# Where two cache copies and fourteen small loads stand in a two-layer decoder kernel

## The reference

```
layer 0: x += [conv module | gated delta rule](rmsnorm(x)) @ w_out_ab     # w_in_ab: 1024 x 3080
         x += PEER(rmsnorm(x))          # 8 heads, 16 of 16384 experts each, rows gathered from a table
         x += sigmoid(rmsnorm(x) @ w_gate) * (p @ w_emb)
layer 1: x += dilated_attention(rmsnorm(x)) @ w_out_c                     # 3 window groups, w_in_c: 1024 x 9216
         x += PEER(...); x += gate(...)
outputs: y, the conv and delta states, and for each window group the rolled key/value cache:
         bufs.append(concatenate([cache, kv_new])[:, L + T - keep:])
```

## Time and profile before

| what | value |
|---|---|
| median of 3 runs | 2553.03 us |
| profiled execution | 2553.16 us, its span 2551.4 us |
| TensorE matmul busy | 2052.6 us, 80% of the span |
| VectorE busy | 1281.3 us, 50% |
| ScalarE busy | 778.3 us, 31% |
| moved by DMA | 874.97 MB, mean 343 GB/s |
| copies of window 2048, 8 of them | 114.8 us to landing (median) |

### The profile page before, as it was taken

One profiled execution on the slowest core, in us unless ns is written; L12 is line 12 of the kernel. 1 busy time (PEld: TensorE's weight loads), 2 busy tenths in 40 slices (PEclk: granted clock), 3 DMA queues, 4 the chain that ended last, 5 costly groups with the idle time before them and its releaser, 6 DMA issues. The chain is left out here.

```text
span 2551.4 us, 25632 instructions
## 1 busy us (share of the span) xinstructions
PE 2052.6 (80%) x9026; PEld 1023.6 (40%) x9026; DVE 1281.3 (50%) x3157; ACT 778.3 (31%) x2275; POOL 644.4 (25%) x645
## 2 busy tenths in 40 slices
PE   5975796478887898877689999987887887988766
PEld 4764684253222243322244565454532222432222
DVE  0076653164776667765511031123556677666754
ACT  0143100023444344443411121121234444344443
POOL 0000000024443444434201000000344444454341
PEclk8987775789999999999789999999899999999978
DMA  6794999669999999999938755753899999999995
GB/s 208 265 336 155 330 329 339 246 263 392 427 427 427 427 427 411 427 427 427 421 151 321 273 206 205 286 206 124 326 427 427 427 427 427 427 425 427 427 427 246
DMA packets 129427, 874.97 MB, mean 343 GB/s; under 512 B 15876, under 2 KB 29700, under 8 KB 45195
## 3 DMA queue, kind: packets, MB, share of 16 engines
q0 software_dynamic: 92160, 662.74, 62.5%
q1 hardware_dynamic: 37139, 210.60, 23.3%
HBM read 861.98 MB, written 118.81 MB: 384 GB/s over the span
## 5 line engine op out<-in xcount | busy, mean ns | idle before, releaser
L1433 PE MATMUL tail_acc<-tail_ring,tail_diag 128*128 128x512 f32 x1216 | 596.8, 621 | 113.1 <-ACT tail_diag L1292 111.9
L1180 DVE CUSTOM_DVE_ANT_0 tail_ring<-tail_ring,all_h 128x1024 f32<-128x1024 f32 x344 | 418.7, 1222 | 239.8 <-DMA tail_ring<-in_peer_uv,tail_idx 239.3
L1573 POOL DMA_INDIRECT mid_wring<-in_peer_uv,tail_idx x232 | 239.1, 1031 | 1005.8 <-DVE all_x L1065 528.7
L1433 PE MATMUL tail_acc<-mid_wring,tail_diag 128*128 128x512 f32 x832 | 413.3, 624 | 98.7 <-ACT tail_diag L1292 98.4
L1573 POOL DMA_INDIRECT tail_ring<-in_peer_uv,tail_idx x344 | 368.7, 1072 | 478.6 <-PE tail_acc L1433 412.8
L1433 PEld LDWEIGHTS tail_acc<-tail_ring,tail_diag 128*128 128x128 f32 x1216 | 216.4, 192 | 478.3 <-ACT tail_diag L1292 298.1
L1180 DVE CUSTOM_DVE_ANT_0 mid_wring<-mid_wring,all_h 128x1024 f32<-128x1024 f32 x232 | 283.3, 1223 | 175.0 <-DMA mid_wring<-in_peer_uv,tail_idx 173.5
L1286 ACT ACTIVATE tail_gelus<-tail_dots 128x1 f32<-128x1 f32 x576 | 116.2, 202 | 723.7 <-DVE tail_dots L1180 723.5
L1433 PEld LDWEIGHTS tail_acc<-mid_wring,tail_diag 128*128 128x128 f32 x832 | 147.8, 193 | 352.9 <-ACT tail_diag L1292 223.0
L1684 PE MATMUL mix_acc<-mid_wring,all_hT 128*128 128x512 f32 x576 | 273.2, 609 | 1.5 <-PEq L80 1.4
L1292 ACT ACTIVATE tail_diag<-all_ident,tail_weights 128x128 f32<-128x128 f32 x512 | 205.5, 401 | 26.8 <-PE tail_acc L1433 9.9
(11 more groups left out here) (363 smaller groups left out, 2083.3 us busy)
## 6 DMA issues: line engine op xcount, KB each, us to landing
mid_wring<-in_w_qkv SPq DMA_DIRECT2D x18, 2048.0 KB, 8.5
out_kv_s<-in_cache_kv_w SPq DMA_DIRECT2D x8, 4064.0 KB, 49.5
mix_ring<-in_kT POOLq DMA_DIRECT2D x16, 1024.0 KB
mix_ring<-in_v_rows POOLq DMA_DIRECT2D x16, 1024.0 KB
ab_ring_w<-in_w_in_ab SPq DMA_DIRECT2D x6, 2048.0 KB, 11.1
mix_ring<-in_kT POOLq DMA_DIRECT2D x16, 768.0 KB, 9.2
mix_ring<-in_v_rows POOLq DMA_DIRECT2D x16, 768.0 KB, 9.2
mid_wring<-in_w_out SPq DMA_DIRECT2D x4, 2048.0 KB, 10.5
```

Source lines behind the costliest of these rows:

```text
L1180: V.tensor_tensor_reduce(out=u, in0=u, in1=h[:, g, :], scale=1.0, scalar=0.0, op0=ALU.mult, op1=ALU.add, accum_out=dots[:, n:n + 1]).then_ ...
L1433: last = mm(acc[g][:, c * 512:(c + 1) * 512], diag[:, n % DIAGS, :], v[:, c * 512:(c + 1) * 512], start=first, stop=final)
L1573: pool.indirect_dma_start(slot(r), None, table, bass.IndirectOffsetOnAxis(ap=idx[:, j, i:i + 1], axis=0)).then_inc(landed[r], 16)
```

## The change

Three things move.

- The 14 inputs of the delta rule are no longer issued at the end of `first_norm_phase` but at the head of SP's stream in `columns_phase`, ahead of the chunk loads there.
- `delta_phase` issues six copies of window 2048 instead of eight.
- The two left out (samples 6 and 7) are cut into 16 pieces of 128 rows, 1 MB each. `dilated_phase` issues one behind each of the 16 weight chunks that it loads. They count on a semaphore of their own, for which the last block waits.

```diff
-def first_norm_phase(nc, K, T, hT, ahead, later):
+def first_norm_phase(nc, K, T, hT, ahead):
                 for to, frm, landed in ahead:
-                    sp.dma_start(to, frm).then_inc(landed, 16)
-                for to, frm, landed in later:
                     sp.dma_start(to, frm).then_inc(landed, 16)
...
-def linear_phase(nc, name, xT, w, width, rows, consume, on="vector", ahead=None, after=None):
+def linear_phase(nc, name, xT, w, width, rows, consume, on="vector", ahead=None, before=(), after=None):
             def _(sp):
+                for to, frm, landed in before:
+                    sp.dma_start(to, frm).then_inc(landed, 16)
                 for c in range(ring if ahead else 0, len(chunks)):
...
-                roll_cache(sp, T, 2, cache_out)
+                roll_cache(sp, T, 2, cache_out, range(DEC_B - LATE))
...
+LATE = 2
...
+                late = roll_pieces(T, 2, range(DEC_B - LATE, DEC_B), 128)
                 for c in range(18):
                     store(3 * c)
                     store(3 * c + 1)
                     sp.wait_ge(product_ready, 3 * c + 3)
                     if c < 16:
                         sp.dma_start(wring[:, c % 2], T["w_qkv"][:, c + 2]).then_inc(w_in[c % 2], 16)
+                        to, frm = late.pop(0)
+                        sp.dma_start(to, frm).then_inc(late_out, 16)
                     else:
                         sp.dma_start(wring[:, c % 2], T["w_out1"][:, c % 2]).then_inc(w_out_in[c % 2], 16)
                     store(3 * c + 2)
...
-                first_norm_phase(nc, K, T, hT, W.start, delta_loads)
+                first_norm_phase(nc, K, T, hT, W.start)
...
-                columns_phase(nc, "ab", hT, T["w_in_ab"][0], IN_AB - 8, zT, ahead=W, after=copies)
+                columns_phase(nc, "ab", hT, T["w_in_ab"][0], IN_AB - 8, zT, ahead=W, before=delta_loads, after=copies)
...
-                sp.wait_ge(cache_out, 16 * NG * DEC_B)
+                sp.wait_ge(cache_out, 16 * (NG * DEC_B - LATE))
+                sp.wait_ge(late_out, 16 * len(roll_pieces(T, 2, range(DEC_B - LATE, DEC_B), 128)))
+
+
+def roll_pieces(T, gi, samples, rows):
+
+    src, dst = T[f"cache_kv_w{PATTERNS[gi][0]}"][0], T[f"out_kv{gi}_s"][0]
+    keep = dst.shape[1] - DEC_T
+    drop = src.shape[1] - keep
+    flat = lambda ap: ap.rearrange("r k h e -> r (k h e)")
+    return [(flat(dst[b, r:min(r + rows, keep)]), flat(src[b, drop + r:drop + min(r + rows, keep)]))
+            for b in samples for r in range(0, keep, rows)]
```

More of the change, by code:

```diff
@@ L298, in linear_phase, with columns_phase @@
                 block.scalar(take)
-def columns_phase(nc, name, xT, w, width, outT, ahead=None, after=None):
+def columns_phase(nc, name, xT, w, width, outT, ahead=None, before=(), after=None):
     def consume(eng, c, part, acc):
         return nc.scalar.activation(outT[:, c * 4 + part, :], acc[:, 0:NTOK], ACT.Copy)
-    linear_phase(nc, name, xT, w, width, False, consume, on="scalar", ahead=ahead, after=after)
+    linear_phase(nc, name, xT, w, width, False, consume, on="scalar", ahead=ahead, before=before, after=after)
 def conv_phase(nc, name, K, T, zT, mixT, conv, cache_out):
@@ L1586, with dilated_phase @@
 UNITS = [(j, it) for it in range(2) for j in range(HH)]
-def dilated_phase(nc, K, T, wring, w_in, mixT, w_out_in):
+LATE = 2
+def dilated_phase(nc, K, T, wring, w_in, mixT, w_out_in, late_out):
     hT, h, ident = K["hT"], K["h"], K["ident"]
@@ L2245, in _ @@
                 sp.wait_ge(x_in, 96)
-        cache_out = P.sem("cache_out")
+        cache_out, late_out = P.sem("cache_out"), P.sem("late_out")
         with ExitStack() as c2:
@@ L2267, in build @@
             tail_phase(nc, K, T, 0, wring, [(wring[:, c], T["w_qkv"][:, c], w_in[c]) for c in range(2)])
-            dilated_phase(nc, K, T, wring, w_in, mixT, w_out_in)
+            dilated_phase(nc, K, T, wring, w_in, mixT, w_out_in, late_out)
             tail_phase(nc, K, T, 1, wring, (), w_out_in)
```

## The result

The changed kernel takes 2539.07 us (median of 7 runs, 2532.52 to 2542.27) against 2554.97 us before (7 runs, 2549.06 to 2558.11): ratio 0.9941, 95% interval 0.9929 to 0.9954, that is 12 to 18 us less. The forecast was 17.3 us less, 2535.9, and its range 2525 to 2546 holds the median.

A forecast was written before the change was run, and what follows sets the result against it. Bounds: SP's issuing in the opening, state stores queued behind copies at the delta rule's end, TensorE in attention. -14.4 - 12.1 + 9.2 = -17.3 us against 2553.16 gave 2535.9 us, range 2525 to 2546.

The forecast's parts named there:

- Step 1: Opening: with the delta inputs issued later, ScalarE's last copy ends it and products start at 21.4 instead of 35.87, -14.4 us.
- The 2.1 us: First product after the opening: time lost to TensorE's low clock after idling, kept as lost; at best it comes back.
- Step 2: End of the delta rule: with two copies fewer, state stores find an empty queue and VectorE ends the phase, -12.1 us.
- my own 406.8 for six copies: Delta rule: predicted landing time of the sixth copy, at 25.2 us per copy, 24 us before the first sample store.
- Step 3: Attention stage: three of the 16 pieces meet full DMA and cost TensorE 3.05 us each, +9.2 us; the others cost nothing.
- the three places named: Attention stage: loads of chunks 3 and 12, amid refills of cached keys, and chunk 7, amid values; 3.05 us each.
- 3.05: Attention stage: the us one 1 MB piece holds the DMA engines, charged to TensorE where refills leave no slack.
- the recorded waits: Attention stage: TensorE's waits for cached keys and values, 6.7 us in sum, predicted to rise to about 16.
- the falling clock: Attention stage, slower rival: seven pieces each cost 3.05 us waiting plus 2.1 us to a low clock, 2563 us; chance 0.04.
- a full stretch: Attention stage: beside chunks 3 to 8 and 12 to 17, cached keys and values are refilled with DMA at 0.88.
- the row of copies 3.0 us apart: Trace evidence for a piece's cost: queued 992 KB copies land 3.0 us apart, preferred over the skill's 6.15 us.
- the ring: Attention stage: four slots that POOL refills with cached keys and values; predicted to have no slack, so pieces there delay TensorE.

The follow-up runs named there:

- the bare placement of 8: Changed kernel with one copy late instead of two, its 8 pieces behind chunks 0, 1, 2, 5, 9, 10, 11 and 14; 0.9886 of the kernel before.
- the opening-only run: Kernel before with only the delta rule's inputs moved out of the opening; all eight copies stay in the delta rule; 0.9941 of the kernel before.
- The second run: Kernel before with only the two copies moved, one piece behind each weight chunk; delta inputs stay in the opening; 0.9979 of the kernel before.
- the third: Changed kernel with its 16 pieces two each behind chunks 0, 1, 2, 5, 9, 10, 11 and 14; 0.9874 of the kernel before.

## Why the prediction was right, step by step

- *Step 1, -14.4 us.* Measured -14.9 in the trace and -15.1 in time by itself. The opening ended with ScalarE, as read, and the first chunk had landed. Of the 0.4 us beyond the forecast, ScalarE's last copy came 0.3 earlier (the phase itself began 0.35 earlier) and the products followed it after 0.68 instead of 0.82. The moved issues cost nothing: from the products' start to the first cache copy it is 48.9 us, 49.1 before. The 2.1 us that the forecast kept as lost to the low clock were lost (2.0), but the record does not show a low clock there (last section), so the number was right and its reason stays open.
- *Step 2, -12.1 us.* The tail started 27.45 us earlier, of which 12.3 are from VectorE's end on: the phase's end trails VectorE by 1.0 us instead of the 13.3 of before. The phase as a whole is 11.1 us shorter, not 12.1, since VectorE's end came 1.1 us later after its start than before. The stores had landed by 424, 13 us before VectorE's last instruction ended. With seven copies the result is the same, and I could have seen that the second late copy was not needed: my own 406.8 for six copies plus 25.2 is 432, 1 us after the first store's issue, so the stores would still have landed some 10 us before VectorE's end.
- *Step 3, +9.2 us.* The stage is 9.9 longer, at exactly the three places named, and the other twelve gaps did not move. Each of the three grew by 3.3 to 4.5 us rather than 3.05, 11.2 in sum. That the stage grew by no more is luck: from the last chunk load to the tail it took 1.6 us less than before, with a granted clock of 0.98 instead of 0.94, and this stretch lasted from 89.3 to 95.0 us in the runs with the same work. The rise of the recorded waits, 6.8 us, is less than the forecast 9.2, and 4.8 us are slower products. Here the prediction had something wrong: it set the falling clock aside because the clock had stayed at 1.00 from 1350 to 1405 us of the kernel before; with the pieces it fell to 0.95 and 0.94 in the three gaps. The two misses, fewer waits and slower products, partly cancel in the sum. That a piece costs about its own DMA time inside a full stretch (3.3 to 3.7 us, slower products included, against the 3.05 estimated) and nothing outside is shown by three placements of the 16 pieces, by the bare placement of 8, and by the run without any.
- *What was weighed from the Trainium skill* ("DMA: Bandwidth & Descriptors", section "Measured (HBM→SBUF, 128 partitions, SWDGE, issued from GpSimd)"), 6.15 us for a load of 1 MB, would have made the three pieces cost 18.5 us. They cost 11.2 together; the row of copies 3.0 us apart was the nearer one.
- *Left open:* the convolutions lasted 116.9 to 123.9 us in runs with the same instructions in that phase (119.0 in the changed kernel, 123.4 in the opening-only run, with a mean granted clock of 0.78 against 0.73). Why it differs from run to run was not tried. The second run beat its expectation by 3 us and the third by 6; such a spread could hide that much, but in the traces of these two the phase lasts 119.6 us in both, so it is not shown to be the reason.

## What to carry to other kernels

At the end of a phase, ask of each store that it waits for which transfers stand in front of it, and cut only as much of them as VectorE's last instruction needs: one copy of 8 MB too many cost 12 us here. A bulk copy moved under a busy stage is free or costs about its whole DMA time according to the stretch that it meets; "38% idle on the mean" hid stretches where the engines were full, and choosing eight other chunks for the same 16 pieces was worth 11.5 us of the stage. Look for issues at a phase's end that nothing in it needs: the next phase can issue them under its own work.

## What the runs showed that I had not expected

- A queue of its own did not protect small stores from large copies: 268 packets of some 500 bytes passed in 25 us beside 130 of 59 KB, 1.8% of the engines' time, and one issue held the issuing engine for 22.7 us.
- Where TensorE waited longer on the ring, its granted clock was lower: 1.00 before, 0.94 to 0.95 in the three gaps of the changed kernel, 0.81 in the 44 us after chunk 3 with five pieces there.
- The first product after the opening took from 4.2 to 7.2 us in different runs (the later ones take 3.88). With the changed kernel's 5.9 us, and even with 7.2, the record of the granted clock says 1.00 from 15 to 30 us, while only 6 of the matmul records fall into 21 to 24 us and 13 into the next three:

```profile
21.00:24.00 3.00, 2.98 (x6) 2.17 (x7) 0.00 (x0) 0.00 (x0) 0.00 (x0) 1.00 1.05 408
24.00:27.00 3.00, 3.00 (x13) 2.35 (x12) 0.00 (x0) 0.15 (x1) 0.00 (x0) 1.00 1.06 412
```

  In the kernel before, 7 records in 36 to 39 us went with a recorded 0.50. So after the change TensorE went at half its later pace for some microseconds while the record says 1.00. Whether the record misses a low clock there or something else slowed the product is open; TensorE's pace tells more than the record does at this place.
